# Neighbourhood-attention items on four PSUM slots, normalised after the merge, put back to token order through HBM

## The chip, the cores and the metric

One core of one Trainium2 chip. The metric is the device time of one execution in microseconds, the slowest core's; here there is one core.

## The reference, cut to what matters

A two-layer encoder on 1024 tokens of width 1024, in float32. In each layer 16 heads of 64 mix the tokens: six dense heads (A), six dilated banded heads (B) and four heads of neighbourhood attention (C) over a grid of 16 rows x 64 columns. Then come the output projection and an MLP of width 4096. The C heads are what the change is about:

```python
sc = jnp.einsum('bnmiphd,bnmjqhd->bnmhipjq', qg, kg, preferred_element_type=jnp.float32) * (d ** -0.5)
sc = sc + bias.transpose(1, 2, 0, 3, 4, 5, 6).astype(jnp.float32)[None]
sc = jnp.where(mask[:, :, None][None], sc, NEG_INF)
p = jax.nn.softmax(sc.reshape(shp[:-2] + (k_rows * NA_KCOLS,)), axis=-1).reshape(shp)
o = jnp.einsum('bnmhipjq,bnmjqhd->bnmiphd', p.astype(v.dtype), vg)
```

## The kernel before

Per layer there are four stages: norm and projections (TensorE matmuls of L1181, whose outputs are transposed and stored to HBM as `feats`, and `values`), the attention, the output projection, and the MLP (L1356 and L1371). float32 operands are split into a high and a low part.

**Attention.** HEADS (L81) gives the order: A, C, A, C, A, C, A, C, then A, A and six B. Each head n has eight items of 128 queries, so item i belongs to head i // 8; four items are a block b. All engines run the same loop over steps i, shifted (TensorE L1315, DVE L974, ACT L709). The text calls A "dense" and C "grid".

- TensorE at step i: scores of item i into PSUM banks 0 to 3, two banks per item (L1245 grid, L1254 others), after the exponential of item i - 2 has read its banks; transposes of item i - 2 (L1271) into banks 4 and 5; a quarter of the weighing of values of a block, from step 4b + 6 (L1293 grid, L1300 others) in bank 6 or 7; at step 4b + 11 the merge of high and low halves (L1311, four matmuls, or eight for the two blocks of a grid head together).
- DVE at step i: for a dense item the negated maximum (L981); for a grid item the custom add-and-minimum with the negated bias tile (L993), which gives minus the maximum. For the grid item i - 1 it then waits for the exponential and scales `prob` by one over the sum (L999 to L1002, 384 columns). Then the low halves of the transposes of item i - 2 (L831 from L1010), and at step 4b + 12 the merged block into `O` (L1024 copy of a whole grid head, L1028 to L1030 scaling of 256 columns for others).
- ACT at step i: high halves of the transposes (L718), exponential (L728), and at step 4b + 9 the eviction of the weighed block into `oT` (L741; for grid blocks two permuting copies, L749, that bring columns back to token order, and a drain).
- POOL: after its value stores, for each bias half-tile (128 x 1536) the negation in place (L552 to L556).

The grid's q features and scores are negated by the scale at L655.

**SyncE's queue** (L510 to L514) issues DMAs in program order and waits in that order too. load_head(n) is for head n: `load_features` (six loads L400, L402 after the scores of head n - 2; for dense heads four more, L408), for a grid head the first half bias (L386), `load_values` (one load L418 or, for a grid head, sixteen L427, after head n - 2 was weighed), and the second half bias. Head n + 1's features come behind that. TensorE waits for all features of a head before its first score (L1231); DVE waits for a half bias tile before its first and its fifth grid item (L989).

```python
                if kind == "C":
                    load_bias(l, 2 * (h - HA - HB))
                load_values(l, n)
                if kind == "C":
                    load_bias(l, 2 * (h - HA - HB) + 1)
```

Of the kernel before, what the change touches and what calls it, by code (L numbers as in the profile page):

```python
# [5 lines left out]
P = 128  # L6
DEPTH = 2
SEQ = 1024
DM = 1024
DFF = 4096  # L10
HD = 64
# [77 lines left out]
GRID_BEFORE = [sum(kind_ == "C" for kind_, _, _ in ITEMS[:n_]) for n_ in range(NI)]  # L89
GROUPS = []  # L90
# [100 lines left out]
def encoder(nc, x_in, wstream, gains, lat_gains, cos_in, sin_in, bias_b, bias_c, ident_in, pair_in, out):  # L191
# [5 lines left out]
    x_park = nc.dram_tensor("x_park", [ST, P, DM], f32).ap()  # L197

# [36 lines left out]
    eps = sb("eps", [P, 1], f32, "STAT", 192)  # L235
    a_nm = sb("a_nm", [P, NI], f32, "STAT", 256 + 512)
# [13 lines left out]
    biasC = [sb("biasC0", [P, 4, CW], f32, "HN"), sb("biasC1", [P, 4, CW], f32, "WS", 56 * KB)]  # L250
    tabB = sb("tabB", [P, 1920], f32, "LAT")
# [6 lines left out]
    with ctx:  # L258
# [28 lines left out]
        biasc_neg = sem("biasc_neg")  # L287
        biasc_in = [sem(f"biasc_in{k}") for k in range(2)]
        s_done, mx_ready, p_ready, pn_ready = sem("s_done"), sem("mx_ready"), sem("p_ready"), sem("pn_ready")
# [46 lines left out]

        def by_block(ap):
            return ap.rearrange("p (b r c) -> p b r c", r=2, b=4)
# [5 lines left out]
        def _(sp):  # L344
# [196 lines left out]
        def _(pool):  # L541

            pool.memset(eps[:, :], EPS).then_inc(eps_set, 1)
            for l in range(DEPTH):
# [7 lines left out]
                for half in range(2 * HC):  # L552
                    pool.wait_ge(biasc_in[half % 2], (l * HC + half // 2 + 1) * 16)
                    hold(pool)
                    bias = biasC[half % 2][:, :, :]
                    pool.tensor_scalar(bias, bias, -1.0, None, ALU.mult).then_inc(biasc_neg, 1)  # L556


        @block.scalar
        def _(act):  # L560
# [61 lines left out]
            for l in range(DEPTH):  # L622
# [4 lines left out]
                for e in EVENTS:  # L627
# [4 lines left out]
                    elif e[0] == "acc":  # L632
# [16 lines left out]
                        elif kind in ("uq", "uk", "cqk"):  # L649
# [4 lines left out]
                            if kind == "cqk":  # L654
                                act.activation(dst[:, 0:wd // 2], bank[:, 0:wd // 2], ACT.Copy, scale=-HD ** -0.5)  # L655
# [53 lines left out]
                for i in range(NI + 8):  # L709
                    if 2 <= i < NI + 2:  # L710
                        it = i - 2
# [9 lines left out]
                    if i < NI:  # L721
                        kind = ITEMS[i][0]
                        wd = CW if kind == "C" else SEQ
# [3 lines left out]
                        s_in = ps[:, 2 * (i % 2):2 * (i % 2) + 2, :].rearrange("p a b -> p (a b)")[:, 0:wd]  # L727
                        act.activation(prob[:, i % 2, 0:wd], s_in, ACT.Exp, bias=a_nm[:, i:i + 1],  # L728
                                       scale=1.0 if kind == "A" else -1.0,
                                       accum_out=a_den[:, i:i + 1]).then_inc(p_ready, 1)  # L730
                    if i == NI:
                        use_table(ACT.Sqrt)
                    if i >= 9 and (i - 9) % 4 == 0 and (i - 9) // 4 < NB:
                        b = (i - 9) // 4
                        act.wait_ge(pv_done, l * NB + b + 1)
                        kind = ITEMS[4 * b][0]
                        if kind != "C":
                            if b >= 2:
                                after_grid = b % 2 == 0 and ITEMS[4 * b - 4][0] == "C"
                                act.wait_ge(mg_done, l * NMG + merges_before(b if after_grid else b - 1))  # L740
                            act.activation(oT[:, (b % 2) * 512:(b % 2 + 1) * 512], ps[:, 6 + b % 2, :], ACT.Copy)\  # L741
                               .then_inc(ot_ready, 1)
                        else:
                            act.wait_ge(mg_done, l * NMG + merges_before(b - b % 2))
                            for c in range(2):
                                cb = 2 * (b % 2) + c
                                src = ps[:, 6 + b % 2, c * 256:(c + 1) * 256].rearrange("p (r c) -> p r c", c=16)
                                dst = oT[:, :].rearrange("p (r c) -> p r c", c=GRID_W)[:, :, 16 * cb:16 * cb + 16]
                                act.activation(dst, src, ACT.Copy)  # L749
                            act.drain().then_inc(ot_ready, 1)  # L750
                act.wait_ge(o_ready, (l + 1) * NMG)

# [70 lines left out]
        def _(dve):  # L823
# [74 lines left out]
            for l in range(DEPTH):  # L898
# [75 lines left out]
                for i in range(NI + 12):  # L974
                    if i < NI:
                        kind, h, q = ITEMS[i]
                        wd = CW if kind == "C" else SEQ
                        dve.wait_ge(s_done, l * NI + i + 1)
                        s_in = ps[:, 2 * (i % 2):2 * (i % 2) + 2, :].rearrange("p a b -> p (a b)")[:, 0:wd]
                        if kind == "A":  # L980
                            dve.tensor_reduce(a_nm[:, i:i + 1], s_in, axis=AX.X, op=ALU.max, negate=True)\  # L981
                               .then_inc(mx_ready, 1)
                        else:
                            if kind == "B":
                                dve.wait_ge(tab_in, (l + 1) * 16)
# [553 lines left out]
```

## Time and profile before

| | |
|---|---|
| median of 3 runs | 2979.0 us (2977.97 to 2985.87) |
| the profiled execution | 2986.88 us |
| its span, first to last instruction | 2985.1 us |
| TensorE matmul busy | 2872.7 us (96%) |
| DVE, ACT, POOL busy | 1753.1, 1057.6, 92.0 us |
| mean granted TensorE clock | 0.985 |
| DMA | 281.11 MB, 94 GB/s |

Busy is the time in which an engine works on an instruction; matmuls are pipelined, so a busy TensorE is not one at its peak, and at the lower of its two clocks (1.2 instead of 2.4 GHz) it is busy longer for the same work. A granted clock of 0.92 is the mean over a stretch in which it was partly 0.5. The profiled execution is one of its own, 7.9 us above the median.

### The profile page before, as it was taken

To read this page: it belongs to the slowest core of one execution; us is meant where nothing else is said; L and a number is where in the kernel's file an instruction comes from. 1 tells how busy PE (TensorE), PEld (TensorE's weight loads), DVE (VectorE), ACT (ScalarE), POOL (GpSimd) and SP (SyncE) were. 2 spreads that over 40 slices of the span, in tenths; PEclk is the share of its full clock that TensorE was granted. 3 is DMA by queue.
4 is the path that set the end of the run, shared out by engine and by line. 5 is a ranking of instruction groups with operands and counts; after the bars stand their busy time and mean duration, and the time that the engine had idled before them with its cause. 6 is when DMAs were issued, how large, how long until landed. Compare 5 with 4: busy or idle time off the path is not lost.

```text
span 2985.1 us, 39896 instructions
## 1 busy us (share of the span) xinstructions
PE 2872.7 (96%) x14640; PEld 2450.0 (82%) x14640; DVE 1753.1 (59%) x3038; ACT 1057.6 (35%) x1992; POOL 92.0 (3%) x69
## 2 busy tenths in 40 slices
PE   7999899998999999999998989999899999999998
PEld 7998778887888888888798977788788888888887
DVE  5642787885554555455666337878755555455457
ACT  5332666774311111111234235678732111111113
POOL 0000210000000000000000011200000000000000
PEclk9999999999999999999999999999999999999999
DMA  5656755413111111111146576543130111111111
GB/s 192 184 180 171 173 145 119 97 39 120 43 43 42 56 42 56 42 42 63 49 174 197 168 188 153 145 94 93 48 113 29 57 42 56 42 42 56 42 61 68
DMA packets 194007, 281.11 MB, mean 94 GB/s; under 512 B 47184, under 2 KB 153296, under 8 KB 184144
## 3 DMA queue, kind: packets, MB, share of 16 engines
q1 hardware_dynamic: 190032, 262.56, 30.6%
q0 software_dynamic: 3840, 16.78, 1.5%
q8 instruction: 81, 1.33, 0.2%
q14 instruction: 54, 0.44, 0.1%
HBM read 208.50 MB, written 70.78 MB: 94 GB/s over the span
## 4 chain that ended last, share of the span: by engine, by line
PE 82%; DVE 7%; issue 3%; DMA 3%; ACT 2%; DVEq 1%; SPq 1%; ACTq 0%; POOL 0%; POOLq 0%
PE ps L1356 23%; PE ps L1181 20%; PE ps L1371 18%; PE ps L1254 6%; PE ps L1271 5%; PE ps L1300 5%; PE ps L1311 2%; PE ps L1149 1%; DVE prob L1001 1%; DMA biasC<-in_bias_c 1%; PE ps L1218 1%; DVE x L1102 1%; DVE pT L831 1%; DMA values<-vst 1%; DVE hn L848 1%
## 5 line engine op out<-in xcount | busy, mean ns | idle before, releaser
L1371 PE MATMUL ps<-w_dn,hid 128*128 128x512 f32 x3072 | 712.9, 391 | 1.4
L1356 PE MATMUL ps<-hT,w_up 128*128 128x512 f32 x3072 | 702.5, 390 | 3.3 <-DVE hT L831 3.3
L1371 PEld LDWEIGHTS ps<-w_dn,hid 128*128 128x128 f32 x3072 | 573.8, 188 | 131.7 <-DVE x L1102 14.1
L1356 PEld LDWEIGHTS ps<-hT,w_up 128*128 128x128 f32 x3072 | 576.4, 188 | 122.9 <-ACT rbuf L781 3.7
L1181 PE MATMUL ps<-ws,hT 128*128 128x384 f32 (+3 forms) x3072 | 606.4, 356 | 2.7 <-issue 1.6
L1181 PEld LDWEIGHTS ps<-ws,hT 128*128 128x128 f32 x3072 | 535.6, 190 | 48.2 <-issue 2.4
L1102 DVE TENSOR_TENSOR x<-ps,x 128x512 f32<-128x512 f32 x512 | 342.7, 689 | 223.6 <-PE ps L1371 223.4
L718 ACT ACTIVATE pT<-ps 128x512 fp32r<-128x512 f32 (+1 forms) x448 | 240.6, 581 | 190.4 <-PE ps L1271 187.3
L1089 DVE TENSOR_TENSOR vbuf<-rbuf 128x512 f32<-128x512 f32 x128 | 88.6, 692 | 371.0 <-ACT rbuf L781 371.0
L831 DVE TENSOR_TENSOR pT<-ps,pT 128x512 fp32r<-128x512 f32 (+1 forms) x448 | 281.5, 664 | 13.8 <-ACT pT L718 13.8
L781 ACT ACTIVATE rbuf<-ps 128x512 f32<-128x512 f32 x128 | 76.6, 598 | 553.9 <-PE ps L1356 553.9
L1271 PE MATMUL ps<-ident,prob 128*128 128x128 f32 x1728 | 238.0, 277 | 35.6 <-DVE prob L1001 19.8
L1271 PEld LDWEIGHTS ps<-ident,prob 128*128 128x128 f32 x1728 | 202.3, 142 | 78.2 <-DVE prob L1001 30.6
L728 ACT ACTIVATE prob<-ps,a_nm 128x1024 f32<-128x1024 f32 (+1 forms) x256 | 252.2, 985 | 36.5 <-DVE a_nm L993 18.9
L767 ACT ACTIVATE w_dn<-raw 128x2048 fp32r<-128x2048 f32 x32 | 61.3, 1917 | 555.8 <-PE ps L1371 555.8
L1300 PE MATMUL ps<-pT,head 128*128 128x512 f32 x768 | 233.8, 429 | 1.8 <-DVE pT L831 1.8
L1254 PE MATMUL ps<-head 128*128 128x512 f32 x768 | 228.7, 399 | 6.9 <-DVEq L942 4.7
L1254 PEld LDWEIGHTS ps<-head 128*128 128x128 f32 x768 | 139.9, 190 | 36.4 <-DVEq L942 5.5
L1300 PEld LDWEIGHTS ps<-pT,head 128*128 128x128 f32 x768 | 136.5, 198 | 21.6 <-DVE pT L831 4.0
L981 DVE TENSOR_REDUCE a_nm<-ps 128x1 f32<-128x1024 f32 x96 | 117.3, 1222 | 44.0 <-PE ps L1254 43.7
L993 DVE CUSTOM_DVE_ANT_0 ps<-ps,tabB 128x1024 f32<-128x1024 f32 x96 | 118.1, 1230 | 37.8 <-PE ps L1254 35.7
L1149 PE MATMUL ps<-ident,hn 128*128 128x128 f32 x448 | 69.5, 305 | 42.4 <-DVE hT L831 21.1
(84 smaller groups left out, 2142.8 us busy)
## 6 DMA issues: line engine op xcount, KB each, us to landing
raw<-in_wstream SPq DMA_DIRECT2D x76, 1024.0 KB, 4.9
head<-feats SPq DMA_DIRECT2D x192, 256.0 KB, 6.1
feats<-tst SPq DMA_DIRECT2D x128, 192.0 KB, 2.5
values<-vst POOLq DMA_DIRECT2D x32, 384.0 KB, 3.1
head<-values SPq DMA_DIRECT2D x24, 512.0 KB, 4.0
biasC<-in_bias_c SPq DMA_DIRECT2D x16, 768.0 KB, 7.7
raw<-in_wstream SPq DMA_DIRECT2D x12, 768.0 KB, 6.0
x_park<-x SPq DMA_DIRECT2D x16, 512.0 KB, 9.3
```

The costliest lines, as they stand in the source:

```text
L718: act.activation(pT[:, b % 2, HI, k0:k0 + nk, (it % 4) * P:(it % 4 + 1) * P], ps[:, 4 + g % 2, 0:nk * P].rearrange("p (k s) -> p k s", s=P ...
L728: act.activation(prob[:, i % 2, 0:wd], s_in, ACT.Exp, bias=a_nm[:, i:i + 1], scale=1.0 if kind == "A" else -1.0, accum_out=a_den[:, i:i + ...
L831: return dve.tensor_tensor(out_lo, full, words(hi), ALU.subtract)
L981: dve.tensor_reduce(a_nm[:, i:i + 1], s_in, axis=AX.X, op=ALU.max, negate=True)\
L993: dve.tensor_tensor_reduce(out=s_in, in0=s_in, in1=bias, scale=1.0, scalar=-NEG, op0=ALU.add, op1=ALU.min, accum_out=a_nm[:, i:i + 1])\
L1102: dve.tensor_tensor(x[:, s, cols], ps[:, 2 + m % 4, :], x[:, s, cols], ALU.add)\
L1181: last = pe.matmul(out_, a, b, start=(n == 0), stop=(n == len(mms) - 1))
L1254: last = pe.matmul(ps[:, b0 + kh, :], a, b, start=(k == 0), stop=(k == len(mm) - 1))
L1271: last = pe.transpose(ps[:, 4 + g % 2, j * P:(j + 1) * P], prob[:, i % 2, c:c + P], ident[:, :])
L1300: last = pe.matmul(bank, hb[:, 4096 + kt * P:4096 + (kt + 1) * P], pT[:, b % 2, w, kt, :], start=(part == 0 and kt == 0 and w == 0), stop= ...
L1356: last = pe.matmul(ps[:, k % 2, :], w_up[0 if first else 1][:, w1, kt, ft * P:(ft + 1) * P], hT[:, w2, kt, sh * 512:(sh + 1) * 512], start ...
L1371: last = pe.matmul(ps[:, 2 + m % 4, :], hid[slot][:, w1, ft, s * P:(s + 1) * P], w_dn[1 if last_group else 0][:, w2, ft, nh * 512:(nh + 1) ...
```

## The change

Grid items take one PSUM bank each and half a `prob` slot each, so that four are in flight; `SLOT_BEFORE` names the item whose place item i takes over (i - 4 within a grid head, i - 2 elsewhere). The steps of transposes, weighing, eviction and merge are those of before. The bias tile and the scale keep their sign, DVE takes the maximum and negates the 128 x 1 result; POOL no longer negates tiles. `prob` is not normalised; each block is merged on its own and scaled by one over the sums as the other kinds are, into `oC` (block order). SyncE stores a finished grid head from `oC` to `grid_out` in HBM by eight DMAs (`park_grid`, in load_head of two heads later, between values and second bias half) and reads it back in token order by one (`read_grid`, in load_head of three heads later, after the features).

```diff
+STEPS = NI + 12
+TURN_STEP = [n_ + 2 for n_ in range(NI)]
+WEIGH_STEP = [TURN_STEP[4 * b_ + 3] + 1 for b_ in range(NB)]
+def turned_at(step):
+    return [i for i in range(NI) if TURN_STEP[i] == step]
+def weighed_at(step):
+    return [(b, step - WEIGH_STEP[b]) for b in range(NB) if 0 <= step - WEIGH_STEP[b] < 4]
+def blocks_at(step):
+    return [b for b in range(NB) if WEIGH_STEP[b] + 3 == step]
+def slots(i):
+    return [2 * (i % 2) + i // 2 % 2] if ITEMS[i][0] == "C" else [2 * (i % 2), 2 * (i % 2) + 1]
+SLOT_BEFORE = [max([m_ for m_ in range(n_) if set(slots(m_)) & set(slots(n_))], default=-1) for n_ in range(NI)]
...
+    grid_out = nc.dram_tensor("grid_out", [HC, SEQ, HD], f32).ap()
+    oC = [sb("oC0", [P, 8, HD], f32, "HN", 6 * KB), sb("oC1", [P, 8, HD], f32, "LAT", 7680)]
...
@@ SyncE, load_head
                 load_features(l, n)
+                if n >= 3 and HEADS[n - 3][0] == "C":
+                    read_grid(l, HEADS[n - 3][1] - HA - HB)
                 if kind == "C":
                     load_bias(l, 2 * (h - HA - HB))
                 load_values(l, n)
+                if n >= 2 and HEADS[n - 2][0] == "C":
+                    park_grid(l, n - 2)
                 if kind == "C":
                     load_bias(l, 2 * (h - HA - HB) + 1)
+            def park_grid(l, n):
+                k = HEADS[n][1] - HA - HB
+                sp.wait_ge(o_ready, l * NB + 2 * n + 2)
+                rows = grid_out[k].rearrange("(f r c) d -> f r c d", f=2, c=GRID_W)
+                for t in range(8):
+                    cb, hf = t // 2, t % 2
+                    sp.dma_start(rows[hf, :, 16 * cb:16 * cb + 16, :], oC[k % 2][:, t, :]).then_inc(grid_parked, 16)
+            def read_grid(l, k):
+                h = HA + HB + k
+                sp.wait_ge(grid_parked, (l * HC + k + 1) * 8 * 16)
+                sp.dma_start(O[:, :, h * HD:(h + 1) * HD], grid_out[k].rearrange("(t p) d -> p t d", p=P))\
+                  .then_inc(grid_back, 16)
@@ GpSimd
-                for half in range(2 * HC):
-                    pool.wait_ge(biasc_in[half % 2], (l * HC + half // 2 + 1) * 16)
-                    hold(pool)
-                    bias = biasC[half % 2][:, :, :]
-                    pool.tensor_scalar(bias, bias, -1.0, None, ALU.mult).then_inc(biasc_neg, 1)
@@ ScalarE
-                                act.activation(dst[:, 0:wd // 2], bank[:, 0:wd // 2], ACT.Copy, scale=-HD ** -0.5)
+                                act.activation(dst[:, 0:wd // 2], bank[:, 0:wd // 2], ACT.Copy, scale=HD ** -0.5)
...
-                        if i >= 2:
-                            act.wait_ge(t_done, l * NGR + ITEM_GROUPS[i - 2][-1] + 1)
+                        if SLOT_BEFORE[i] >= 0:
+                            act.wait_ge(t_done, l * NGR + ITEM_GROUPS[SLOT_BEFORE[i]][-1] + 1)
...
-                            for c in range(2):
-                                ...
-                                act.activation(dst, src, ACT.Copy)
-                            act.drain().then_inc(ot_ready, 1)
+                        if b >= 2:
+                            act.wait_ge(mg_done, l * NB + b - 1)
+                        act.activation(oT[:, (b % 2) * 512:(b % 2 + 1) * 512], ps[:, 6 + b % 2, :], ACT.Copy)\
+                           .then_inc(ot_ready, 1)
+                act.wait_ge(o_ready, (l + 1) * NB)
+                act.wait_ge(grid_back, (l + 1) * HC * 16)
@@ VectorE, grid items
-                                dve.wait_ge(biasc_neg, l * 2 * HC + n4 + 1)
+                            dve.wait_ge(biasc_in[n4 % 2], (l * HC + n4 // 2 + 1) * 16)
                             hold(dve)
+                            dve.tensor_tensor_reduce(out=score(i), in0=score(i), in1=biasC[n4 % 2][:, q % 4, :],
+                                                     scale=1.0, scalar=NEG, op0=ALU.add, op1=ALU.max,
+                                                     accum_out=a_mx[:, i:i + 1])
+                            dve.drain()
+                            dve.tensor_scalar(a_nm[:, i:i + 1], a_mx[:, i:i + 1], -1.0, None, ALU.mult)\
                                .then_inc(mx_ready, 1)
-                    if 1 <= i <= NI and ITEMS[i - 1][0] == "C":
-                        it = i - 1
-                        dve.wait_ge(p_ready, l * NI + it + 1)
-                        dve.reciprocal(a_rd[:, it:it + 1], a_den[:, it:it + 1])
-                        dve.drain()
-                        dve.tensor_scalar(prob[:, it % 2, 0:CW], prob[:, it % 2, 0:CW], a_rd[:, it:it + 1], None,
-                                          ALU.mult).then_inc(pn_ready, 1)
@@ VectorE, after the merge of a block
                         if kind == "C":
-                            dve.tensor_copy(O[:, :, cols],
-                                            ps[:, 6 + b % 2, :].rearrange("p (t d) -> p t d", d=HD))\
-                               .then_inc(o_ready, 1)
+                            o = oC[h % 2][:, q:q + 4, :]
+                            done = l * HC + h - HA - HB - 1
+                            if done > 0:
+                                dve.wait_ge(grid_parked, done * 8 * 16)
+                        dve.reciprocal(a_rd[:, 4 * b:4 * b + 4], a_den[:, 4 * b:4 * b + 4])
+                        dve.drain()
+                        dve.tensor_tensor(o, ps[:, 6 + b % 2, 0:4 * HD].rearrange("p (t d) -> p t d", d=HD),
+                                          a_rd[:, 4 * b:4 * b + 4].unsqueeze(2).to_broadcast([P, 4, HD]),
+                                          ALU.mult).then_inc(o_ready, 1)
@@ TensorE
-                    if i >= 2:
-                        pe.wait_ge(p_ready, l * NI + i - 1)
+                    if SLOT_BEFORE[i] >= 0:
+                        pe.wait_ge(p_ready, l * NI + SLOT_BEFORE[i] + 1)
-                    b0 = 2 * (i % 2)
+                    b0 = slots(i)[0]
...
-                    if kind == "C":
-                        pe.wait_ge(pn_ready, l * 8 * HC + GRID_BEFORE[i] + 1)
-                    else:
-                        pe.wait_ge(p_ready, l * NI + i + 1)
+                    pe.wait_ge(p_ready, l * NI + i + 1)
...
-                    for k in range(8 if kind == "C" else 4):
-                        c = k * P + (0 if kind == "C" else (b % 2) * 512)
+                    for k in range(4):
+                        c = k * P + (b % 2) * 512
```

## Rows read from the trace of the kernel before

**Rows 1.** The page: the span, and the chain that ended last, by engine.

```profile
span 2985.1 us, 39896 instructions
...
PE 82%; DVE 7%; issue 3%; DMA 3%; ACT 2%; DVEq 1%; SPq 1%; ACTq 0%; POOL 0%; POOLq 0%
```

**Rows 2.** Grid heads: length, busy PE, PEld, DVE, ACT, POOL, clock, DMA share, GB/s.

```profile
309.40:334.80 25.40, 19.28 (x99) 15.67 (x99) 17.04 (x44) 12.19 (x30) 8.17 (x2) 0.87 0.72 163
358.90:378.20 19.30, 16.08 (x99) 13.12 (x98) 13.68 (x43) 10.96 (x28) 4.31 (x1) 1.00 0.80 196
402.30:423.60 21.30, 17.73 (x99) 14.43 (x99) 16.97 (x43) 10.85 (x28) 4.08 (x1) 0.92 0.70 169
447.70:469.80 22.10, 18.91 (x99) 15.71 (x97) 17.07 (x43) 10.77 (x28) 4.08 (x1) 0.85 0.65 162
...
1781.70:1809.70 28.00, 19.76 (x98) 16.66 (x99) 15.57 (x43) 11.42 (x30) 8.17 (x2) 0.82 0.72 157
1833.80:1855.30 21.50, 19.03 (x99) 15.83 (x97) 16.29 (x43) 10.73 (x28) 4.08 (x1) 0.84 0.67 165
1879.50:1899.60 20.10, 17.34 (x98) 14.24 (x97) 16.47 (x43) 10.69 (x28) 4.08 (x1) 0.92 0.71 177
1923.80:1944.00 20.20, 17.41 (x98) 14.29 (x97) 16.50 (x43) 10.70 (x28) 4.08 (x1) 0.92 0.71 175
```

**Rows 3.** Timeline of the first grid head: start us, us, engine, line, instruction, idle before.

```profile
310.43 4.08 POOL L556 TENSOR_SCALAR biasC<-biasC 128x1536 f32<-128x1536 f32 x1 [18.81 <-DMA biasC<-in_bias_c]
...
314.68 0.57 DVE L993 CUSTOM_DVE_ANT_0 ps<-ps,biasC 128x384 f32<-128x384 f32 x1 [4.41 <-POOL biasC L556]
...
319.40 4.08 POOL L556 TENSOR_SCALAR biasC<-biasC 128x1536 f32<-128x1536 f32 x1 [4.89 <-DMA biasC<-in_bias_c]
...
320.10 3.60 DVE L1001 TENSOR_SCALAR prob<-prob,a_rd 128x384 f32<-128x384 f32 x1
```

**Rows 4.** Timeline around the grid head that starts at 402.34.

```profile
394.32 7.46 SPq L427 DMA_DIRECT2D head<-values  x16
...
401.83 0.43 SPq L386 DMA_DIRECT2D biasC<-in_bias_c  x1
...
405.17 0.68 DVE L1024 COPY O<-ps 128x512 f32<-128x512 f32 x1
...
405.99 1.98 SPq L408 DMA_DIRECT2D head<-feats  x4
```

**Rows 5.** Issues by line and their landings: L408 three times (third landing only), L386, L489.

```profile
L408 SPq DMA_DIRECT2D head<-feats x4: 421/422/583, 406.0 to 407.5; - x4
...
DMA to landing us min/median/max: 8.3/8.3/8.9
...
L408 SPq DMA_DIRECT2D head<-feats x4: 421/422/582, 314.4 to 315.9; - x4
...
DMA to landing us min/median/max: 9.6/9.7/10.7
...
DMA to landing us min/median/max: 9.1/9.2/10.7
...
DMA to landing us min/median/max: 6.2/6.2/6.2
...
L489 SPq DMA_DIRECT2D feats<-tst x64: 518/627/4012, 229.1 to 1759.2; - x64
...
DMA to landing us min/median/max: 2.0/2.2/9.9
```

**Rows 6.** Timeline of SyncE's queue, first grid head of layer 2.

```profile
1779.37 5.22 SPq L427 DMA_DIRECT2D head<-values  x5
...
1788.80 1.98 SPq L408 DMA_DIRECT2D head<-feats  x4
```

**Rows 7.** Timeline, the dense head after the first grid head.

```profile
343.84 1.16 PE L1271 MATMUL ps<-ident,prob 128*128 128x128 f32 x8 [0.33 <-DVE pT L831]
```

**Rows 8.** Timeline, fifth item's scores of the grid head from 358.9.

```profile
368.25 0.52 PE L1245 MATMUL ps<-head 128*128 128x384 f32 x2
```

More of the change, by code:

```diff
@@ L235, in encoder @@
     eps = sb("eps", [P, 1], f32, "STAT", 192)
+    a_mx = sb("a_mx", [P, NI], f32, "STAT", 256)
     a_nm = sb("a_nm", [P, NI], f32, "STAT", 256 + 512)
@@ L335, in from_grid, with score, probability @@
             return bank[:, j * P:(j + 1) * P].rearrange("p (r b c) -> p b r c", r=2, b=4)
+        def score(i):
+            b0 = slots(i)[0]
+            return ps[:, b0, 0:CW] if ITEMS[i][0] == "C" else ps[:, b0:b0 + 2, :].rearrange("p a b -> p (a b)")
+        def probability(i):
+            c = 512 * (i // 2 % 2) if ITEMS[i][0] == "C" else 0
+            return prob[:, i % 2, c:c + (CW if ITEMS[i][0] == "C" else SEQ)]
         def by_block(ap):
@@ L706, in _ @@
                         turn += 1
-                for i in range(NI + 8):
-                    if 2 <= i < NI + 2:
-                        it = i - 2
+                for i in range(STEPS):
+                    for it in turned_at(i):
                         b = it // 4
@@ L721, in _ @@
                     if i < NI:
-                        kind = ITEMS[i][0]
-                        wd = CW if kind == "C" else SEQ
                         act.wait_ge(mx_ready, l * NI + i + 1)
-                        if i >= 2:
-                            act.wait_ge(t_done, l * NGR + ITEM_GROUPS[i - 2][-1] + 1)
-                        s_in = ps[:, 2 * (i % 2):2 * (i % 2) + 2, :].rearrange("p a b -> p (a b)")[:, 0:wd]
-                        act.activation(prob[:, i % 2, 0:wd], s_in, ACT.Exp, bias=a_nm[:, i:i + 1],
-                                       scale=1.0 if kind == "A" else -1.0,
+                        if SLOT_BEFORE[i] >= 0:
+                            act.wait_ge(t_done, l * NGR + ITEM_GROUPS[SLOT_BEFORE[i]][-1] + 1)
+                        act.activation(probability(i), score(i), ACT.Exp, bias=a_nm[:, i:i + 1],
+                                       scale=-1.0 if ITEMS[i][0] == "B" else 1.0,
                                        accum_out=a_den[:, i:i + 1]).then_inc(p_ready, 1)
@@ L971, in _ @@
                         turn += 1
[L974 removed]
+                for i in range(STEPS):
                     if i < NI:
                         kind, h, q = ITEMS[i]
[L977 removed]
                         dve.wait_ge(s_done, l * NI + i + 1)
[L979 removed]
                         if kind == "A":
[L981 removed]
+                            dve.tensor_reduce(a_nm[:, i:i + 1], score(i), axis=AX.X, op=ALU.max, negate=True)\
@@ L1005, in _ @@
+                    for it in turned_at(i):
                         b = it // 4
@@ L1012, in _ @@
                                  pT[:, b % 2, HI, k0:k0 + nk, cols]).then_inc(t_lo, 1)
-                    if i >= 12 and (i - 12) % 4 == 0 and merged((i - 12) // 4):
-                        b = (i - 12) // 4
+                    for b in blocks_at(i - 3):
                         kind, h, q = ITEMS[4 * b]
@@ L1270, in turns @@
                             c = (4 * k + j) * P
-                            last = pe.transpose(ps[:, 4 + g % 2, j * P:(j + 1) * P], prob[:, i % 2, c:c + P],
+                            last = pe.transpose(ps[:, 4 + g % 2, j * P:(j + 1) * P], probability(i)[:, c:c + P],
                                                 ident[:, :])
@@ L1313, in merge @@
                     last.then_inc(mg_done, 1)
-                for i in range(NI + 12):
+                for i in range(STEPS):
                     if i < NI:
                         scores(i)
-                    if 2 <= i < NI + 2:
-                        turns(i - 2)
-                    if i >= 11 and (i - 11) % 4 == 0 and merged((i - 11) // 4):
-                        merge((i - 11) // 4)
-                    if i >= 6 and (i - 6) // 4 < NB:
-                        weigh((i - 6) // 4, (i - 6) % 4)
+                    for it in turned_at(i):
+                        turns(it)
+                    for b in blocks_at(i - 2):
+                        merge(b)
+                    for b, part in weighed_at(i):
+                        weigh(b, part)
                 norm_turn(l, ST, 0)
@@ L1406 @@
 VALUE_N = [sum(VALUE_DMAS[kd] for kd, _ in HEADS[k::2]) for k in range(2)]
-MERGED = [ITEMS[4 * b][0] != "C" or b % 2 == 1 for b in range(NB)]
-NMG = sum(MERGED)
-def merged(b):
-    return b < NB and MERGED[b]
-def merges_before(b):
-    return sum(MERGED[:b])
 def turn_of(stg):
```

53 lines of the change are left out of this document (15 added, 38 removed).

## The prediction

> **What bounds the kernel now.** I read the page first: TensorE carries most of the chain that ended last, and POOL, ACT and DVE hardly appear in it [rows 1]. A change that takes work off DVE and POOL can therefore only pay where TensorE waits for them. So I next cut the attention into stages, one per grid head, from its first score matmul to the first of the next dense head [rows 2]. Each grid head holds about 16.1 us of TensorE work at full clock (the stage from 358.9 has 16.08 busy at clock 1.00), yet the eight stages last 25.4, 19.3, 21.3, 22.1 and 28.0, 21.5, 20.1, 20.2 us, together 177.9. Some 49 us, the excess over 8 x 16.1, is all that the edit could win in these stages. The dense heads between them are TensorE throughout, with one small stall each [rows 7].
>
> The timeline of the first grid head says what the excess is [rows 3]. The bias tile lands, POOL negates it for 4.08 us, and DVE stands idle 4.41 us for that. Later DVE's scaling of `prob` takes 3.60 us while POOL negates the second tile. DVE works in program order, so TensorE's transposes stop behind both. The first grid head of each layer pays twice, as both tiles arrive during it; the six later ones have their first tile long before, and only the second arrives inside.
>
> That second tile is the hinge. SyncE issues in order: 16 loads of grid values, then this bias tile, then ten loads for the next dense head. For the head that starts at S = 402.3 the values take 7.46 us of issue, the bias goes out at 401.83 (S - 0.5), and the last four loads begin at 405.99 [rows 4]. Those four land 8.3 us after issue, the last at 407.5 + 8.3 = 415.8, or S + 13.5; 14.0 us after the bias was issued [rows 5]. Stages run at a DMA share of 0.65 to 0.80 on average [rows 2], so that chain is transfer, not latency, and moves as one block.
>
> **What the change does, part by part.** Call S the start of a grid head.
>
> *POOL's negation goes* (8 per layer, 4.1 us each). DVE waits for the tile itself. *The normalisation of `prob` goes* from between exponential and transposes: a reciprocal, a drain and the 384-wide scale. What DVE adds is a drain and a 128 x 1 negation after each of 64 maxima; the trace has no such negation. It costs below nothing net if it simply takes the place of the longer pair it replaces, at most some 0.25 us x 64 = 16 us if each one is exposed. I take 0, because DVE's busy time in every such stage is 14 to 17 of 19 to 28 us [rows 2]. If that cover were gone, the transposes would be late. *The merges*: two of four matmuls replace one of eight; DVE scales 256 columns per block where it copied 512 per pair (0.68 us [rows 4]); ACT evicts once instead of twice with a drain. Same TensorE work; I take 0.
>
> *Four deep.* Scores of an item need only the exponential of the fourth before. This lets TensorE run scores ahead, but turns and weighing are still two and six steps behind, so a late bias tile stops it all the same, about two steps later.
>
> *The first grid head of each layer.* Nothing new sits ahead of it in SyncE's queue. Layer 1: the tile is there at 310.4, only 1 us after the head begins; the second at 319.4, when POOL started [rows 3], by then the 13th item is due. TensorE's own work ends at S + 16.1. The next head's last load is issued at 315.9 and lands 9.7 later, 325.6, S + 16.2 [rows 5]. So 25.4 becomes 16.2, minus 9.2. Layer 2: last load issued near 1790.4, landing 9.2 later, S + 17.9 [rows 5, 6]; the late first tile costs TensorE some 2 us and some slow clock, I take 19.2, so 28.0 - 19.2 = 8.8. Together **-18.0**.
>
> *The six later grid heads, and here the change takes back.* In program order of SyncE, eight stores of the previous grid head are put between its values and the second bias tile, behind a wait for that head's last merge. Where is that merge? DVE's copy for it begins at 405.17, S + 2.8, and takes 0.68 [rows 4]: ready at S + 3.5. The scaled version is about as long. Then eight DMAs: 16 value loads of 128 pieces took 7.46, 0.47 each [rows 4], so 3.8 us. The trace has no store of 256-byte pieces. Bounds: stores of 128-byte pieces have a median of 0.63 [rows 5], and under a full queue five value loads took 5.22, 1.04 each [rows 6]; below, 0.43 of a single issue. I take 0.47, since the queue is empty then, after a wait. The bias goes out at S + 7.4 instead of S - 0.5. It lands 6.2 later [rows 5], at S + 13.6, while the fifth item's scores stand at 368.25, S + 9.4 [rows 8]: DVE waits, TensorE loses about 3 us, hidden in what follows. The ten loads follow as a block: last landing at S + 7.4 + 14.0 = **S + 21.4**. The next dense head cannot score before. TensorE's own work would end before that (16.1 plus 3). So the six stages, 19.3 + 21.3 + 22.1 + 21.5 + 20.1 + 20.2 = 124.5, become 6 x 21.4 = 128.4: **+3.9**. The read back is one more issue behind the ten, wanted only at the layer's end: 0 on the path, and 0.4 us of SyncE.
>
> *Clock.* After a wait TensorE's granted clock falls to its lower level: stages with 2 to 3 us of waiting show 0.92, 0.85, 0.84, that is 1.6 to 3.4 us each, one shows 1.00 [rows 2]. Those losses lie inside the old stages. In the new ones part is swallowed by the wait for loads, and part falls on the start of the next dense head. Bounds 0 and 3.4 per head; I take 1.2, **+7**.
>
> *Dense heads after grid heads* (8): the stall before their transposes (0.33 us plus as much again of weight load [rows 7]) comes of DVE being late with a scale that is gone. I take 0.5 each, **-4**; bounds 0 and 0.66 each.
>
> **Sum**: -18.0 + 3.9 + 7 - 4 = -11.1. The profiled execution took 2986.9 (span 2985.1 [rows 1]), so it would become 2975.8. It stands 7.9 above the median of the runs, 2979.0; applied to the median, **2968**.
>
> **Two rules weighed.** DVE's 3.60 us beside POOL's 4.08 us [rows 3] reads as waiting for a port. The Trainium skill (SBUF — State Buffer, on the port pair that DVE and GpSimd share) has it as an exclusive lock held for a whole instruction; by that every long scale vanishes with POOL's work, as in my sum. Against the change: the Trainium skill (DMA: Bandwidth & Descriptors, Specifications) wants pieces of at least 512 B for full rate, and the new stores have 256 B. If such stores ran at half rate, the sum would get worse by up to 4 us per head, 24 in all. The trace does not agree so far: 128-byte stores land in about 2 us once issued [rows 5].
>
> **Rivals.** (1) *The full gain.* The stores leave SyncE early enough, or the loads behind them compress, so the later heads end with TensorE's own work and the wait for the tile, near 18.5: 6 x 18.5 = 111, -13.5 instead of +3.9, clock +3: -18 - 13.5 + 3 - 4 = -32.5, **2946**. For it: POOL and DVE are what the waits name. Against: the block of 14 us behind the bias. (2) *The clock costs more.* The new wait at a dense head's start puts each at the lower level, 3.4 us a head, 20 in place of 7: +1.9 in all, **2981**, not told from no change. For it: 0.84 and 0.85 in two of six [rows 2]. This is also the case in which the change doesn't do what it says: waits are only moved. (3) *Slower: the eight stores hold SyncE's queue.* Each costs 1.04 as in the full queue [rows 6] instead of 0.47: 4.6 us later per head, +27, **2995**. It decides from 0.89 us each (8 x 0.42 x 6 = 20, which turns -11 into +9); up to 0.70 there is still a gain. Against it: the queue is empty at that point.
>
> **How the numbers follow.** Forecast 0.44, rival (1) 0.16, rival (2) 0.26, rival (3) 0.14. A measurement of this kernel tells 0.3% (9 us) from no change. The forecast's own range is 2958 to 2980, some two thirds of it under 2970; with rival (1) that gives faster 0.48; slower is rival (3) and a sliver, 0.15; the rest is same, 0.37. For 8 in 10 the range takes in rival (1) and (2) and half of (3): 2943 to 2990.
>
> **What would show it.** In the changed profile: no POOL `biasC` row, no `prob` row on DVE; first grid heads of 16 to 19 us; in the six later ones SyncE's bias issue near S + 7.4, eight stores of about 0.47 us ahead of it, and the first dense score waiting for "DMA head<-feats" until about S + 21.4. If that wait is absent and stages are near 18, rival (1) holds; if stores take 1 us, rival (3). If the bias issue is still at S - 0.5, or the first heads keep more than 22 us, my reading of the queue is wrong.

## The result, and the profile after

The changed kernel takes 3001.9 us (median of 6 runs, 2998.8 to 3012.7) where the kernel before takes 2978.7 (6 runs): 23 us slower, ratio 1.0075 with a 95% interval of 1.0052 to 1.0098. The forecast was 2968, faster by 0.37%, with a range of 2943 to 2990; the result lies outside it, on the other side of no change.

The page of the changed kernel, its span and its chain, beside [rows 1]:

```profile
span 3010.9 us, 39890 instructions
...
PE 81%; DVE 5%; DMA 5%; issue 3%; SPq 3%; ACT 2%; DVEq 1%; ACTq 0%; POOLq 0%
```

DVE gave 2 points of the chain back, and DMA and SyncE's queue (SPq) took 4. POOL's work is gone. Now the grid heads as stretches, layer 1 then layer 2, columns as in [rows 2]:

```profile
310.20:330.10 19.90, 15.84 (x99) 13.37 (x98) 12.61 (x38) 12.08 (x30) 0.00 (x0) 1.00 1.10 223
355.20:381.00 25.80, 18.58 (x100) 15.67 (x98) 12.35 (x38) 11.18 (x30) 0.00 (x0) 0.83 0.72 159
406.70:432.20 25.50, 18.55 (x99) 15.65 (x97) 12.36 (x38) 11.10 (x30) 0.00 (x0) 0.83 0.72 163
457.90:482.70 24.80, 18.58 (x99) 15.64 (x98) 12.35 (x38) 11.15 (x30) 0.00 (x0) 0.83 0.73 162
...
1796.90:1817.10 20.20, 15.85 (x99) 13.36 (x98) 12.70 (x38) 12.07 (x30) 0.00 (x0) 0.97 1.06 225
1843.20:1867.50 24.30, 18.25 (x100) 15.46 (x99) 12.35 (x38) 11.14 (x30) 0.00 (x0) 0.85 0.73 163
1892.40:1916.50 24.10, 18.55 (x99) 15.65 (x97) 12.36 (x38) 11.09 (x30) 0.00 (x0) 0.83 0.73 162
1942.40:1967.00 24.60, 18.81 (x99) 15.64 (x98) 12.27 (x38) 11.20 (x30) 0.00 (x0) 0.84 0.72 160
```

The first grid head of each layer went from 25.4 and 28.0 us to 19.9 and 20.2, -13.3 together. The six later ones went from 124.5 to 149.1, +24.6: they are 25 us long although DVE works 12.4 us in each and POOL nothing. The timeline around the one that starts at 406.7 shows where they stand (start us, us, engine, line, instruction, idle before):

```profile
409.78 0.42 DVE L1063 TENSOR_TENSOR oC<-ps,a_rd 128x256 f32<-128x256 f32 x1
410.23 4.96 SPq L435 DMA_DIRECT2D grid_out<-oC  x8
...
415.24 0.46 SPq L447 DMA_DIRECT2D biasC<-in_bias_c  x1
...
420.49 2.19 SPq L469 DMA_DIRECT2D head<-feats  x4
422.73 0.42 SPq L441 DMA_DIRECT2D O<-grid_out  x1
423.19 3.65 SPq L479 DMA_DIRECT2D head<-values  x1
423.45 0.57 DVE L1032 CUSTOM_DVE_ANT_0 ps<-ps,biasC 128x384 f32<-128x384 f32 x1 [8.14 <-DMA biasC<-in_bias_c]
...
425.06 0.90 PE L1300 MATMUL ps<-ident,prob 128*128 128x128 f32 x3 [5.57 <-ACT prob L779]
...
432.29 1.22 PE L1286 MATMUL ps<-head 128*128 128x512 f32 x2 [0.70 <-DMA head<-feats]
```

The last merge is stored from 410.23 (S + 3.5), the second bias tile is issued at 415.24 (S + 8.5, before the change S - 0.5 [rows 4]), DVE waits 8.14 us for it and TensorE 5.57 behind DVE; then the next dense head's first score waits for its features until S + 25.6. The landing times of the four last feature loads and of the bias tile, and the issue times of all stores, beside [rows 5]:

```profile
DMA to landing us min/median/max: 7.3/7.4/10.0
...
DMA to landing us min/median/max: 8.0/8.0/8.0
...
L435 SPq DMA_DIRECT2D grid_out<-oC x64: 570/571/717, 358.8 to 2002.3; - x64
```

And the dense head that follows starts with TensorE at its lower clock (columns as above):

```profile
432.20:457.90 25.70, 25.61 (x150) 22.45 (x151) 18.95 (x26) 17.20 (x32) 0.00 (x0) 0.91 0.49 125
432.20:436.20 4.00, 3.91 (x13) 3.25 (x13) 0.94 (x1) 0.30 (x1) 0.00 (x0) 0.50 0.88 209
```

The granted clock is 0.50 in its first 4 us, that is 1.2 GHz, after a grid head in which TensorE was made to wait (5.57 us for the tile, then 0.70 us for the features). Six dense heads between grid heads took 144.5 us before (24.1 each) and 153.3 now (25.1, 25.7, 25.6, 26.1, 24.9, 25.9): +8.8. The two dense heads that follow the last grid heads add 2.7 (24.1 and 24.3 before, 25.4 and 25.7 now). The sum, 24.6 - 13.3 + 8.8 + 2.7 = +22.8, is about the 23 between the medians. The two profiled executions from which the rows come are further apart, 25.8 us (2985.1 and 3010.9); the other 3 us lie outside these stages.

### The profile page after: what moved, and what is told of

Its sections match the earlier page's. It is cut to its first block, busy times and chain, and to the rows that moved or that the text cites. A ratio compares the mean times of both kernels' runs of the same rounds, so it can differ in the third digit from the quotient of the medians.

```text
span 3010.9 us, 39890 instructions
## 1 busy us (share of the span) xinstructions
PE 2890.4 (96%) x14640; PEld 2469.6 (82%) x14640; DVE 1720.6 (57%) x2998; ACT 1056.8 (35%) x1976; POOL 26.3 (1%) x53
## 4 chain that ended last, share of the span: by engine, by line
PE 81%; DVE 5%; DMA 5%; issue 3%; SPq 3%; ACT 2%; DVEq 1%; ACTq 0%; POOLq 0%
PE ps L1384 23%; PE ps L1213 20%; PE ps L1399 17%; PE ps L1286 7%; PE ps L1300 5%; PE ps L1329 4%; DMA head<-feats 3%; PE ps L1339 1%; PE ps L1181 1%; PE ps L1250 1%; DMA values<-vst 1%; SPq L463 1%; DVE x L1134 1%; SPq L488 1%; PE ps L1322 1%
## 5 line engine op out<-in xcount | busy, mean ns | idle before, releaser
L1286 PE MATMUL ps<-head 128*128 128x512 f32 x768 | 239.4, 414 | 18.6 <-DMA head<-feats 11.8
L1329 PE MATMUL ps<-pT,head 128*128 128x512 f32 x768 | 224.1, 414 | 1.8 <-DVE pT L871 1.8
L1329 PEld LDWEIGHTS ps<-pT,head 128*128 128x128 f32 x768 | 130.5, 190 | 20.6 <-DVE pT L871 4.0
L1181 PE MATMUL ps<-ident,hn 128*128 128x128 f32 x448 | 70.3, 307 | 41.2 <-DVEq L890 20.6
```

Source lines behind the costliest of these rows:

```text
L1286: last = pe.matmul(ps[:, b0 + kh, :], a, b, start=(k == 0), stop=(k == len(mm) - 1))
L1329: last = pe.matmul(bank, hb[:, 4096 + kt * P:4096 + (kt + 1) * P], pT[:, b % 2, w, kt, :], start=(part == 0 and kt == 0 and w == 0), stop= ...
```

## Experiments

Theory Q: the loss is the order of SyncE's queue, the tile and the features behind the stores. Rival F: four in flight, or DVE's drain and negation, cost the time. Rival T: the small transfers themselves do. Times are medians, each with the ratio to the kernel before on the same chip; stage lengths are from the one profiled execution of each kernel.

**1. The bias tile ahead of the stores again.**

```diff
                 load_values(l, n)
-                if n >= 2 and HEADS[n - 2][0] == "C":
-                    park_grid(l, n - 2)
                 if kind == "C":
                     load_bias(l, 2 * (h - HA - HB) + 1)
+                if n >= 2 and HEADS[n - 2][0] == "C":
+                    park_grid(l, n - 2)
```

> The changed kernel (3001.9 us), with the second bias tile issued ahead of the eight stores again; the next head's features stay behind them. Theory Q (the loss is the order in SyncE's queue: what stands behind the stores comes late): DVE's 8 us wait for the tile goes, but the next dense head still waits for its features, which are free of 0.77 MB of bias in front: last landing about 3.5 us earlier, so the six later grid heads go from 25.0 to about 21.5 us, -21 in all: 2975 to 2985. Rival F (four items in flight, or DVE's drain and negation, cost the time): nothing changes, over 2995. Rival T (the small transfers themselves slow the other loads): at most a third of the gain, 2990 to 3000.

Measured: 2984.8 us, ratio 1.0021 (1.0010 to 1.0033). The six later grid heads last 20.9 to 22.1 us. The wait for the tile is gone from the stage shown above, and TensorE's idling is now in front of the dense head's first score:

```profile
424.48 1.22 PE L1286 MATMUL ps<-head 128*128 128x512 f32 x2 [5.63 <-DMA head<-feats]
```

So the features are a bound of their own, as Q has it, and the tile only lengthened the block in front of them. Rival F falls; T gave 2990 or more. The dense heads between two later grid heads still last 25.5 to 26.0 us, behind this one wait as behind the two of the changed kernel.

**2. The stores one head later.**

```diff
                 load_features(l, n)
                 if n >= 3 and HEADS[n - 3][0] == "C":
-                    read_grid(l, HEADS[n - 3][1] - HA - HB)
+                    park_grid(l, n - 3)
                 if kind == "C":
                     load_bias(l, 2 * (h - HA - HB))
+                if n >= 4 and HEADS[n - 4][0] == "C":
+                    read_grid(l, HEADS[n - 4][1] - HA - HB)
                 load_values(l, n)
-                if n >= 2 and HEADS[n - 2][0] == "C":
-                    park_grid(l, n - 2)
```

> The changed kernel with the eight stores issued one head later, behind the features of the head after, and the read back one head later still: the same transfers, nothing that is due soon behind them. Theory Q: the six later grid heads end with TensorE's own work, 16.5 to 18 us, and the dense heads start at full clock: 6 x 7.5 + 8 x 1.5 = 57 less than 3001.9, about 2945. Rival T: the stores and read back still run beside loads, 2975 to 2990. Rival F: over 2990.

Measured: **2933.7 us**, ratio 0.9845 (0.9828 to 0.9861), 45 us faster than the kernel before and 68 faster than the change. A later grid head and the dense head behind it, and SyncE's queue in the same stretch:

```profile
392.70:408.20 15.50, 15.40 (x99) 13.31 (x98) 11.88 (x38) 10.56 (x29) 0.00 (x0) 1.00 0.93 220
408.20:431.70 23.50, 23.50 (x153) 20.70 (x152) 19.20 (x27) 17.85 (x34) 0.00 (x0) 1.00 0.70 169
```

```profile
393.09 0.43 SPq L447 DMA_DIRECT2D biasC<-in_bias_c  x1
...
397.25 1.98 SPq L469 DMA_DIRECT2D head<-feats  x4
399.27 6.59 SPq L435 DMA_DIRECT2D grid_out<-oC  x8
```

The stores take longer to issue than in the changed kernel, 6.59 us for eight, and it costs nothing: TensorE is busy 15.40 of 15.50 us at full clock. Same work, same transfers, another place in the queue. The expectation was 11 us too high: it had 16.5 to 18 us for a later grid head, and all six last 15.5 to 15.8.

**3. The stores from GpSimd's queue.** `park_grid` and `read_grid` run in POOL's program, with the same waits, after its value stores; SyncE's queue is that of before.

```diff
...
+                for k in range(HC):
+                    park_grid(l, 2 * k + 1)
+                    read_grid(l, k)
```

> The changed kernel with stores and read back issued from GpSimd's queue, at the same moment as in the changed kernel (right after the last merge), SyncE's queue as before the change. Theory Q: as with the late stores, about 2945, since only SyncE's order is undone. Rival T: the transfers run at the same time as in the changed kernel, so most of the loss stays, 2980 or more. A descriptor written by GpSimd beside DVE's work could cost some us on DVE: then 2950 to 2960.

Measured: 2943.1 us, ratio 0.9877 (0.9861 to 0.9894). Later grid heads last 15.8 to 16.6 us. The transfers run at the moment of the changed kernel, right after the merge, and the loss is gone: T falls. It stays 9 us behind the late stores. In the profiled executions, 11.7 us apart, the six later grid heads hold 4.6 of it (0.8 each) and the two first ones, which scatter from kernel to kernel, 6.2; no run tells why.

**4. No trip.** No stores, no read back, and no waits for them. The blocks go straight into `O` in block order; what is left out is the return of the grid heads to token order.

```diff
...
-                        if kind == "C":
-                            o = oC[h % 2][:, q:q + 4, :]
...
```

> The changed kernel without the stores and the read back: merged grid blocks go straight into O in block order (the grid heads' tokens stay permuted, so this part of the computation is left out). Theory Q and rival T both: about 2943, the floor that the late stores should come within 5 us of by Q, and be 30 above by T. Rival F: over 2990.

Measured: 2937.5 us, ratio 0.9857 (0.9841 to 0.9874), within the scatter of experiment 2. The trip, put late, is free.

**5. The read back one head later**, the stores where the change has them.

```diff
-                if n >= 3 and HEADS[n - 3][0] == "C":
-                    read_grid(l, HEADS[n - 3][1] - HA - HB)
                 if kind == "C":
                     load_bias(l, 2 * (h - HA - HB))
+                if n >= 4 and HEADS[n - 4][0] == "C":
+                    read_grid(l, HEADS[n - 4][1] - HA - HB)
```

> The changed kernel with only the read back moved, one head later, behind that head's first bias tile; the stores stay ahead of the second tile. It asks why the block of loads behind the stores took 17 us from the bias issue to the last landing and not the 14 of before. If the read back's transfer runs among the features and draws them out (theory R): 1 to 1.5 us less per later grid head, some 6 to 9 us, about 2994. If it is the late start itself (SyncE's slower issue, the value load that now follows at once; rival V): unchanged, 2999 to 3004.

Measured: 3003.0 us, ratio 1.0077 (1.0060 to 1.0094): no change from the changed kernel. Theory R falls.

**6. Sixteen stores.**

```diff
...
+                rows = spare[k].rearrange("(f r c) d -> f r c d", f=2, c=GRID_W)
+                for t in range(8):
+                    cb, hf = t // 2, t % 2
+                    sp.dma_start(rows[hf, :, 16 * cb:16 * cb + 16, :], oC[k % 2][:, t, :]).then_inc(grid_parked, 16)
```

> The changed kernel with each of the eight stores issued twice, the second time to a spare tensor. Theory Q has a price: eight more issues of 0.62 us are 5.0 us later for everything behind them, on six grid heads, so +30: about 3032 (3025 to 3040). Rival T (the transfers and not their place): two times 0.25 MB per head at some 220 GB/s is 1.2 us, +7: 3009. If the dense head's features were not what ends the stage: +0 to 5.

Measured: 3034.1 us, ratio 1.0177 (1.0151 to 1.0203), 32 above the changed kernel. The same stretch, a grid head that starts at 410.3; first SyncE's queue, then DVE's and TensorE's waits:

```profile
413.80 4.97 SPq L436 DMA_DIRECT2D grid_out<-oC  x8
418.81 5.20 SPq L440 DMA_DIRECT2D spare<-oC  x8
424.05 0.46 SPq L452 DMA_DIRECT2D biasC<-in_bias_c  x1
```

```profile
431.22 0.57 DVE L1037 CUSTOM_DVE_ANT_0 ps<-ps,biasC 128x384 f32<-128x384 f32 x1 [12.33 <-DMA biasC<-in_bias_c]
...
439.99 1.22 PE L1291 MATMUL ps<-head 128*128 128x512 f32 x2 [0.62 <-DMA head<-feats]
```

The bias goes out 5.2 us later (S + 13.8), and the stage is 29.7 us instead of 25.6. Over the six later grid heads, 174.3 us instead of 149.2, that is 4.2 us each: most of the 5.2 us of issue in front of the block is passed on, six times.

**7. Features alone.** In the changed kernel a dense head's read back and value load wait for that head's first score.

```diff
                 load_features(l, n)
+                if kind == "A" and HEADS[n - 1][0] == "C":
+                    sp.wait_ge(s_done, l * NI + 8 * n + 1)
```

> The changed kernel with the dense head's read back and value load held until that head's first scores are done, so that its features have the DMA engines to themselves; stores, tile and features stay where they are. Rival V (the value load and read back that now follow at once draw the features out): the block takes 14 to 15 us instead of 17, the six later grid heads 22 to 23 instead of 25 us, some -13 to -18: 2984 to 2990. If the 17 us come of the late start alone (0.6 instead of 0.47 us per store, a slower first issue): unchanged, 2999 to 3004.

Measured: 2990.5 us, ratio 1.0033 (1.0022 to 1.0045), 11 us less than the change, just outside of what V gave. Later grid heads last 23.3 to 25.3 us. First a wait in the one that starts at 402.8 and the next head's first score, then, from SyncE's queue, the bias issue in between, and the landings of the four last feature loads (the last one issued at 417.9):

```profile
419.26 0.57 DVE L1034 CUSTOM_DVE_ANT_0 ps<-ps,biasC 128x384 f32<-128x384 f32 x1 [7.83 <-DMA biasC<-in_bias_c]
...
427.20 1.16 PE L1288 MATMUL ps<-head 128*128 128x512 f32 x2
```

```profile
411.36 0.46 SPq L449 DMA_DIRECT2D biasC<-in_bias_c  x1
...
DMA to landing us min/median/max: 7.2/7.4/8.7
```

From the tile's issue at 411.36 to the last landing at 426.64 the block takes 15.3 us here, where the changed kernel took 17.0 in the same stage. Over the six later grid heads it takes 15.2 us in the mean, against 16.2 in the changed kernel: the value load and the read back draw it out by 1.0 us a head. V is right in kind and smaller in size.

In two of the six stages, the one shown among them, the first score no longer waits for features; here it comes at S + 24.4 because TensorE, at the lower clock after its wait for the tile, needs until then. In the other four it still waits 0.2 to 0.9 us for them. So the tile, with the clock after it, stands close behind the features.

**8. Two in flight instead of four**, on the late stores of experiment 2.

```diff
-    return [2 * (i % 2) + i // 2 % 2] if ITEMS[i][0] == "C" else [2 * (i % 2), 2 * (i % 2) + 1]
+    return [2 * (i % 2), 2 * (i % 2) + 1]
```

> The late stores (2933.7 us) with grid items on two banks and two places each as before the change, that is two in flight instead of four. My account says that depth is worth little where no tile comes late, since transposes and weighing keep their steps: 2934 to 2938. Rival D (depth is what the gain comes from): the chain scores, maximum, drain, negation, exponential of some 2.0 us no longer fits in a step of 1.6 us, 0.3 to 0.5 us per item on 64 items: 2950 to 2965.

Measured: 2934.1 us, ratio 0.9849 (0.9833 to 0.9866). The depth, first in the change's name, is worth nothing here that these runs can tell.

**9. POOL negates again**, on the late stores: its `tensor_scalar` on the tiles, DVE's minimum without drain and negation, the scale and the sign of the exponential as before.

```diff
+                    pool.tensor_scalar(bias, bias, -1.0, None, ALU.mult).then_inc(biasc_neg, 1)
...
-                            dve.wait_ge(biasc_in[n4 % 2], (l * HC + n4 // 2 + 1) * 16)
+                            dve.wait_ge(biasc_neg, l * 2 * HC + n4 + 1)
...
-                                                     scale=1.0, scalar=NEG, op0=ALU.add, op1=ALU.max,
-                                                     accum_out=a_mx[:, i:i + 1])
-                            dve.drain()
-                            dve.tensor_scalar(a_nm[:, i:i + 1], a_mx[:, i:i + 1], -1.0, None, ALU.mult)\
-                               .then_inc(mx_ready, 1)
+                                                     scale=1.0, scalar=-NEG, op0=ALU.add, op1=ALU.min,
+                                                     accum_out=a_nm[:, i:i + 1]).then_inc(mx_ready, 1)
```

> The late stores with POOL's negation of the bias tiles put back (and DVE's minimum without drain and negation). Theory P (POOL's 4.1 us ahead of DVE is most of the gain): the first grid head of each layer waits 4 us again, twice, and the six later ones get their second tile at S + 10 instead of S + 6, 0 to 2 us each: +10 to +20, 2944 to 2954. Rival N (the normalisation taken out of prob is most of it): under +6, below 2940.

Measured: 2940.8 us, ratio 0.9867 (0.9851 to 0.9884): +7, between both, though the interval touches that of experiment 2 (0.9828 to 0.9861). The first grid heads are 21.5 and 21.7 us, where experiment 2 has 17.2 and 17.6, so P is right for them; but the six later ones last 15.4 to 16.3, although POOL works in them:

```profile
403.67 4.09 POOL L618 TENSOR_SCALAR biasC<-biasC 128x1536 f32<-128x1536 f32 x1 [12.40 <-DMA biasC<-in_bias_c]
404.51 0.57 DVE L1038 CUSTOM_DVE_ANT_0 ps<-ps,biasC 128x384 f32<-128x384 f32 x1 [0.57 <-PE ps L1280]
404.99 0.14 DVE L1038 DVE_READ_ACCUMULATOR2_ANT a_nm<- 128x1 f32 x1
405.18 0.56 DVE L877 TENSOR_TENSOR pT<-ps,pT 128x384 fp32r<-128x384 f32 x1
...
407.93 0.57 DVE L1038 CUSTOM_DVE_ANT_0 ps<-ps,biasC 128x384 f32<-128x384 f32 x1 [2.20 <-POOL biasC L618]
```

DVE's operations on PSUM keep their length beside POOL, and the 2.20 us that DVE waits for the tile reach nobody.

**10. The sign alone**, on the kernel before: POOL's negation gone, maximum with drain and negation; `prob` normalised, two in flight, no trip.

```diff
...
+                                dve.tensor_tensor_reduce(out=s_in, in0=s_in, in1=bias, scale=1.0, scalar=NEG,
+                                                         op0=ALU.add, op1=ALU.max, accum_out=a_mx[:, i:i + 1])
+                                dve.drain()
+                                dve.tensor_scalar(a_nm[:, i:i + 1], a_mx[:, i:i + 1], -1.0, None, ALU.mult)\
+                                   .then_inc(mx_ready, 1)
```

> The kernel before with only the sign changed: POOL's negation gone, DVE's maximum with drain and negation; prob is still normalised, two items in flight, no trip through HBM. Theory P: DVE is held by POOL's work alone, so the later grid heads come to about 17 us too: 6 x 3.5 + 2 x 8 = 37 less, 2942. Rival N (the normalisation between exponential and transposes costs as much by itself): half of the later heads' gain, 2950 to 2960.

Measured: 2953.5 us, ratio 0.9907 (0.9892 to 0.9922), 11 us above P and inside N's range. By the stages it is nearer to P: the six later grid heads gave back 18.6 us (21 by P, half of that by N), the two first ones 15.8 (16 by P). But the kernel before was profiled in a long execution, so these two figures may be too high. All six later ones last 17.7 to 17.8 us, and DVE's scale of `prob`, 3.60 us beside POOL in [rows 3], never is:

```profile
L1003 DVE TENSOR_SCALAR prob<-prob,a_rd x64: 419/420/425, 313.8 to 1914.5; 128x384 f32<-128x384 f32 x64
```

The remaining 20 us to experiment 2 (18 in the profiled executions) lie mostly in the six later grid heads, 17.7 to 15.5 us, 13 together. Depth and trip are worth nothing (experiments 8 and 4), so what is left is the normalisation moved behind the merge, together with the merge and the eviction per block that come with it; no run takes these apart.

**11. Both tiles early**, on the late stores: the second tile directly behind the first, ahead of the values.

```diff
                     load_bias(l, 2 * (h - HA - HB))
+                    load_bias(l, 2 * (h - HA - HB) + 1)
...
                 load_values(l, n)
-                if kind == "C":
-                    load_bias(l, 2 * (h - HA - HB) + 1)
```

> The late stores (2933.7 us) with the second bias tile issued right behind the first, ahead of the sixteen value loads. The later grid heads are TensorE's own 15.5 us already and can't gain; the first head of each layer (17.2 and 17.6 us) may lose the rest of its wait for the second tile, 1 to 2 us each, unless the values, now 3 us later, are what it waits for next: 2930 to 2935.

Measured: 2933.0 us, ratio 0.9838 (0.9825 to 0.9852). The first grid heads stay at 17.4 and 17.7. Not told from experiment 2.

## Why the prediction was wrong, point by point

**The mechanism was read right.** The hinge was SyncE's order, the merge was ready at S + 3.5 as said (409.78 + 0.42), the first dense score waits for its features, and rival (3) named this queue as the way to slower. Experiments 2 and 6 show it from both sides: 68 us less with the stores out of the way, 32 more with twice as many.

**The term that failed is the six later grid heads**, +3.9 forecast, +24.6 measured. The forecast had the last features at S + 21.4; they land at S + 24.8 in the mean, and in all six stages the first dense score follows at once. It was built of three numbers. Ready at S + 3.5: right. Eight stores at 0.47 us: they cost 0.62 (4.96 for eight), and the tile goes out at S + 8.6 in the mean instead of S + 7.4, 1.2 us a head. I took the value loads as the nearest row because they too have 128 pieces, where the stores in [rows 5], 0.63, were nearer: store to store, although those have 512 pieces of 128 B. The block of 14.0 us from the bias issue to the last landing: it took 17.1, 17.0 and 16.2 in layer 1 and 15.6, 15.6 and 15.8 in layer 2, 16.2 in the mean, 2.2 more. Together 3.4 us a head, 20.6 in six, and 20.7 were missed.

Of the 2.2 us, 0.7 was a misreading: 8.3 in [rows 5] is the median of four landings, and the last load, which is the one that counts, took the maximum, 8.9; the block of before was 14.7 us in the mean of the six. Another 1.0 I moved "as a block" and forgot what stands behind it. Before, the dense head's value load had to wait for a weighing and came 12 us after the last feature load (419.9 against 407.5); a block that is 9 us late has it at its heels, and experiment 7 shows the price. The last 0.5 us stays open.

**Clock and dense heads**: +7 and -4 were forecast, together +3; measured +8.8 in six and 11.5 in eight. The lower clock did land on the dense head's start (0.50 for 4 us). Where the grid head ends without a wait, the small stall and the lower clock are both gone: 23.5 us in experiment 2. Against that a dense head between grid heads now lasts 25.6 us, so the clock costs 2.1 us a head, where I took 1.2. One wait is enough for it: experiment 1 has only the one for features, 5.0 to 6.5 us, and the dense heads between two later grid heads are as long, 25.5 to 26.0 us.

**The first grid heads**, -18.0 forecast, -13.3 measured. In layer 1 the next head's features landed at S + 19.9, not S + 16.2: their last load was issued at S + 7.4 instead of S + 6.5 and took 12.4 us. The 9.7 of the forecast is again a median; the last load took 10.7 already before [rows 5]. The second tile was issued 1 us later too, in a part of the queue that no edit touched. These stages scatter from kernel to kernel: 15.3 to 21.3 us among the experiments in which POOL doesn't negate and `prob` isn't normalised, so with one profiled execution each, some of the 4.7 us is chance.

With 20.7, 4.7 and 8.5 us (11.5 - 3) the three terms make the 33.9 us between forecast and result.

**Four deep**: taken at nothing, and nothing it is (experiment 8). The negation on DVE, 0.15 us each, is hidden: the later grid heads of experiment 2 have it and last 15.5 us, TensorE's own time. That is also less than the 16.1 us that I took for TensorE's work; no run tells why. The merges per block cost nothing that shows in those stages, but were not tested by themselves.

**Rivals.** (1), the full gain, was priced at 2946 and is real once the queue is in order: 2934. (2) had the right place, the dense head's start; there it priced 16 us (20 - 4) and 11.5 were measured, but it left the queue as forecast. (3) had the right place and the wrong price: 1.04 us per store was too much. By its own rule a store of up to 0.70 us still gives a gain, and 0.62 gave a loss, because what lengthens the block was not in it; that its 2995 comes within 7 us of the result is luck. The upper end of the range held either the clock or half of the queue, never both, and they are not independent: with the stores out of the way the later grid heads and the dense heads behind them are at clock 1.00 (experiment 2).

**The rules.** DVE's long scale beside POOL as a port lock held for a whole instruction (the Trainium skill, SBUF — State Buffer, Who interferes with whom): the trace agrees. The kernel before has seven long scales, 2.75 to 3.81 us, and each ends 0.21 us after POOL's negation does (in [rows 3] 320.10 + 3.60 against 319.40 + 4.08); experiment 10, without POOL, has 425 ns at most. The rule on pieces of at least 512 B for full rate (the Trainium skill, DMA: Bandwidth & Descriptors, Specifications) did not decide: the 256-byte stores cost nothing when nobody due stands behind them. Their rate itself was not measured, and the 2 us of landing that the prediction held against the rule is not a rate either.

## What to carry to other kernels

A DMA put into an in-order queue costs what stands behind it, not what it moves: before adding one with a wait, list the transfers behind it with the moment each is due, and put it behind the last that is due soon. When a block of loads slides late, also look at what used to come long after it, and at the clock of TensorE after the new wait; these losses come together. And test the parts of a combined change one by one: here 28 us lay in a sign, about 20 in the moved normalisation with its merges, none in the depth, and a loss of 68 in the place of eight stores. When a row gives the median and the maximum of several landings, ask which of them the waiting engine needs: it is the last.

## What the runs showed of the hardware that I had not expected

A store of 128 pieces of 256 B holds SyncE's queue 0.57 us and 0.62 with its gap, a load of 128 pieces of 512 B 0.43 and 0.47. GpSimd's queue issued the same eight stores of a grid head in 4.79 us, about the same pace. Of DVE's operations beside POOL's negation only the 384-wide scale from SBUF to SBUF is held (0.42 us alone, up to 3.81 beside POOL). The maximum and the subtraction, with one input from PSUM, keep their 0.57 and 0.56 us, and so does the 128 x 1 reciprocal in the kernel before, 0.16 us, although it too reads and writes SBUF only.
